# VectorE's order in the gated feed-forward loops: the product of gate and up half first, then the low part of the next weights, then the product's low part, then the side step

## The reference, cut to what matters

```
def swiglu(a, w13, w2):
    gate, up = jnp.split(a @ w13, 2, axis=-1)
    return (jax.nn.silu(gate) * up) @ w2
...
        mod = c_act @ ada_w[l] + ada_b[l]
        (sh1, sc1, gt1, sh2, sc2, gt2, sh3, sc3, gt3) = jnp.split(mod, N_ADA, axis=-1)
        f = swiglu_2(modulate_2(rmsnorm(h, ln_ffn1[l]), sh1, sc1), ffn1_wg[l], ffn1_wu[l], ffn1_wd[l])
```

## Time and profile before

| what | value |
|---|---|
| median of 3 runs | 2943.21 us (2938.38 to 2951.15) |
| the profiled execution | 2962.52 us |
| its span in the trace | 2961.2 us |
| PE busy | 2783.0 us, 94% of the span |
| DVE busy | 2008.7 us, 68% |
| ACT busy | 1226.4 us, 41% |
| POOL busy | 340.5 us, 11% |
| mean granted TensorE clock | 0.967 of full speed |
| mean transfer rate | 177 GB/s |

### The profile page before, as it was taken

How to read it: one execution, slowest core, us unless ns; L and a number is a source line. 1 busy time by engine, 2 the same in 40 slices (tenths; PEclk the granted TensorE clock), 3 DMA queues, 4 the chain that set the end, 5 groups by cost and what they waited for, 6 DMA issues and landing times.

```text
span 2961.2 us, 61219 instructions
## 1 busy us (share of the span) xinstructions
PE 2783.0 (94%) x26612; PEld 2633.2 (89%) x26612; DVE 2008.7 (68%) x2888; ACT 1226.4 (41%) x1634; POOL 340.5 (11%) x332
## 2 busy tenths in 40 slices
PE   7999998999999998988999989999999998989999
PEld 5888886999998777987999888999999998988998
DVE  5787776777776787677656865676565577647654
ACT  2323224445444334434544432555454444144643
POOL 5000001202011121003110020021020101000301
PEclk9999998999999998998998999999999999999999
DMA  8355353899996776998656622456576664233664
GB/s 291 115 188 162 107 172 101 243 257 283 256 267 190 209 232 190 264 285 220 185 166 163 158 73 87 115 157 185 166 200 173 176 165 107 87 103 119 178 168 132
DMA packets 747401, 525.17 MB, mean 177 GB/s; under 512 B 19370, under 2 KB 711788, under 8 KB 747004
## 3 DMA queue, kind: packets, MB, share of 16 engines
q1 hardware_dynamic: 741808, 515.87, 60.8%
q0 software_dynamic: 4128, 5.06, 0.6%
q10 hardware_dynamic: 1196, 0.32, 0.0%
HBM read 520.07 MB, written 2.94 MB: 177 GB/s over the span
## 4 chain that ended last, share of the span: by engine, by line
PE 40%; DVE 9%; ACT 6%; issue 5%; DMA 1%; POOL 0%; DVEq 0%; SPq 0%; ACTq 0%; POOLq 0%
PE bank L519 11%; PE bank L520 11%; PE bank L521 11%; ACT weights_hi L487 4%; DVE weights_lo L498 2%; DVE conv_out L2374 1%; PE bank L2548 1%; PE bank L2540 1%; PE bank L2552 1%; PE bank L1520 1%; PE bank L548 1%; DMA weights_raw<-in_ffn_w 1%; DVE side_sums_odd L620 0%; DVE side_sums L620 0%; DVE conv_out L2371 0%
## 5 line engine op out<-in xcount | busy, mean ns | idle before, releaser
L498 DVE TENSOR_TENSOR weights_lo<-weights_raw,weights_hi 128x2048 fp32r<-128x2048 f32 (+3 forms) x414 | 852.8, 2060 | 367.9 <-ACT weights_hi L487 367.6
L487 ACT ACTIVATE weights_hi<-weights_raw 128x2048 fp32r<-128x2048 f32 (+3 forms) x414 | 709.7, 1715 | 596.9 <-PE bank L521 479.7
L519 PE MATMUL bank<-ffn_in_hi,weights_hi 128*128 128x256 f32 x1184 | 340.9, 288 | 28.1 <-DVE ffn_prod L1388 17.5
L520 PE MATMUL bank<-ffn_in_lo,weights_hi 128*128 128x256 f32 x1184 | 334.2, 282 | 0.0
L521 PE MATMUL bank<-ffn_in_hi,weights_lo 128*128 128x256 f32 x1184 | 333.9, 282 | 0.0
L519 PE MATMUL bank<-mix_in_hi,weights_hi 128*128 128x256 f32 x960 | 280.5, 292 | 11.0 <-DVE conv_in L2404 4.4
L519 PE MATMUL bank<-mac_in_hi,weights_hi 128*128 128x256 f32 x1024 | 288.5, 282 | 2.2 <-DVE mac_prod L2157 1.7
L520 PE MATMUL bank<-mac_in_lo,weights_hi 128*128 128x256 f32 x1024 | 287.6, 281 | 0.0
L521 PE MATMUL bank<-mac_in_hi,weights_lo 128*128 128x256 f32 x1024 | 287.6, 281 | 0.0
L520 PE MATMUL bank<-mix_in_lo,weights_hi 128*128 128x256 f32 x960 | 272.7, 284 | 0.0
L521 PE MATMUL bank<-mix_in_hi,weights_lo 128*128 128x256 f32 x960 | 272.3, 284 | 0.0
(11 more groups left out here) (437 smaller groups left out, 7008.0 us busy)
## 6 DMA issues: line engine op xcount, KB each, us to landing
weights_raw<-in_ffn_w SPq DMA_DIRECT2D x132, 512.0 KB, 6.4
weights_raw<-in_w_in SPq DMA_DIRECT2D x120, 512.0 KB, 5.1
side_weights<-in_ada_w SPq DMA_DIRECT2D x86, 576.0 KB, 4.4
weights_raw<-in_ffn_wg SPq DMA_DIRECT2D x88, 512.0 KB, 4.0
weights_raw<-in_ffn_wu SPq DMA_DIRECT2D x88, 512.0 KB, 5.3
weights_raw<-in_ffn_wd SPq DMA_DIRECT2D x64, 704.0 KB, 4.6
weights_raw<-in_ffn_w SPq DMA_DIRECT2D x48, 704.0 KB, 7.2
side_weights<-in_ada_w SPq DMA_DIRECT2D x112, 256.0 KB, 3.2
```

The costliest lines, as they stand in the source:

```text
L487: k.s.activation(k.w_hi[i % HIGHS][:, 0:n], k.raw[s % RING][:, 0:n], ACT.Copy).then_inc(*k.hi.up())
L498: k.v.tensor_tensor(k.w_lo[s % RING][:, 0:n], k.raw[s % RING][:, 0:n], k.w_hi[i % HIGHS][:, 0:n].bitcast(F32), ALU.subtract).then_inc(*k.l ...
L519: k.te.matmul(out, l[0], r[0], start=first, stop=False)
L520: k.te.matmul(out, l[0], r[1], start=False, stop=False)
```

## The change: what it does

Two loops of VectorE change their order; no instruction is added or removed, and the other engines' queues stay as they are. In `dve_ffn_up` an iteration was: low part of the weights, side steps, product, product's low part. It becomes: product, low part of the weights, product's low part, side steps. In `dve_macaron` the same is done from iteration 6 on, without side steps; iterations 0 to 5 keep their order.

```
 def dve_ffn_up(k, sides, other):
     v = k.v
     for i in range(KF):
-        dve_lo(k)
-        for _ in range(sides.up[i]):
-            dve_side(k)
         v.wait_ge(*k.gated.at(i + 1))
         v.wait_ge(*k.mid_lo.at(i - 1))
         v.tensor_tensor(k.prod[i % 2][:, :], k.gate[i % 2][:, :], k.GB[ffn_turn(k, i) % 2][0][:, T:2 * T],
                         ALU.mult).then_inc(*k.ev.up())
+        dve_lo(k)
         v.wait_ge(k.ev.h, ffn_turn(k, i) + 1)
         v.wait_ge(*k.mid_hi.at(i + 1))
         v.tensor_tensor(k.mid[1][:, i, :], k.prod[i % 2][:, :], k.mid[0][:, i, :].bitcast(F32),
                         ALU.subtract).then_inc(*k.mid_lo.up())
+        for _ in range(sides.up[i]):
+            dve_side(k)
         if i in sides.up_end:
             dve_side_finish(k, sides.up_end[i], k.GB[0][1])
...
     for i in range(KF):
-        dve_lo(k)
+        if i < LATE:
+            dve_lo(k)
         if i == 0:
             dve_rms(k)
...
         if i >= LATE:
             v.wait_ge(*k.gated.at(i + 1))
             v.tensor_tensor(x, g, bank[1][:, 0:T], ALU.mult).then_inc(*k.ev.up())
+            dve_lo(k)
             v.wait_ge(k.ev.h, turn + 1)
             v.wait_ge(*k.mid_hi.at(i + 1))
             v.tensor_tensor(k.mid[1][:, i, :], x, k.mid[0][:, i, :].bitcast(F32), ALU.subtract).then_inc(*k.mid_lo.up())
```

## The result

The changed kernel takes 2906.86 us (median; 2899.46 to 2908.98), the kernel before 2941.16 us beside it: ratio 0.987, 95% interval 0.9846 to 0.9895, a gain of 34 us by the medians and of 38 by the ratio. A later comparison of the same two gave 0.9885 (0.9864 to 0.9907), 33 us. The recorded forecast was 2919 us, a gain of 24: the sign and the first block as the place were right, but the gain is some 40% larger than said, and 2906.86 lies just outside the range (2907 to 2938).

What follows compares the result with a forecast made beforehand. A chain between VectorE and ScalarE, 0.67 us longer than TensorE's 5.44, bounds the first block's slow stretches. Gains of 6.4, 7.1, 5.3 and 5.1 make 24 us: 2943.2 - 24 = 2919 us, range 2907 to 2938.

Steps and rivals of the forecast that it cites:

- The ring of 6.11 us: First block's up loops: VectorE and ScalarE hand one chain back and forth, 6.11 us per iteration against TensorE's 5.44.
- Rival 1: First block's up loops: transfers hold the old pace at 265 GB/s, gaining only 3.8 us, 2939 us; chance 0.17.
- Rival 2: First block: only TensorE's visible waits for the product, 17.5 us, come back, 2926 us; chance 0.09.
- Rival 3: First block: new ring over three iterations is longer if landings exceed 10.5 us; 19 us slower, 2962 us; chance 0.06.
- third layer, double, 4 slabs: End of third layer's up loop, two side steps per iteration: 6.4 us a slab instead of 7.68, gaining 5.1 us.
- third layer, 7 slabs "gain nothing": Third layer stretch where TensorE already runs at 5.44 us a slab, 38.08 us in all: no gain.
- the transfers 6.4: Third layer's double side steps: 2.23 MB per iteration takes 6.4 us at 350 GB/s, taken as each slab's time.
- VectorE's bound 6.06: Third layer's double side steps: VectorE's instruction durations per iteration add up to 6.06 us.
- I cost this half of the change at nothing: Second block: low part was done before SiLU anyway and TensorE has no wait worth naming, so gain 0.
- rival 4: Second block also falls into the faster pace: 17 us on top of the forecast, 2902 us; chance 0.05.
- the middle of 5.44 and 5.71: TensorE's pace without waits in the first block's single-side-step stretches: 5.575 us a slab, both ends giving the range.
- To some 0.1 us each: First block: ScalarE's wait for the product was to fall from 3.4 us to this per iteration.

Runs made afterwards that it cites:

- e3: Kernel before, with only the first block's side step moved behind the product's low part; weights' low part stays ahead of the product: 2911.49 us, ratio 0.9895.

## Why the prediction was wrong by 12 us

Two of the 12 us are not the change's: the kernel before measured 2943.2 us when the forecast was made and 2941.16 beside the result. As a gain the range was 5 to 36 us and 34 lies inside it; in the later comparison the changed kernel's median was 2914.28. That 2906.86 falls just outside the range rather than just inside is chance. That the middle was 10 us too small is not.

**What held.** The ring of 6.11 us was the cause: taking only the side step out of it gives the gain, within the intervals (e3). TensorE's wait for the product vanished, and the list of waits shows the ring cut. *Rival 1* (transfers hold the pace) fell: the four stretches run at 277 to 315 GB/s, above the 265 it named, and TensorE has no wait for weights in them. *Rival 2* (only the visible 17.5 us) fell: the four stretches gave 29.5. *Rival 3* fell: ScalarE's waits for raw weights rose from 87.0 to 126.5 us in the whole span, but none reaches TensorE. One landing took 10.8 us (500 to 650 us, median 6.5), longer than the 10.5 at which this rival was to decide; a single one did no harm. The bound from the transfers does exist, as the layout with more double side steps shows.

**The terms of the sum**, in the two profiled executions:

| term | forecast (ends) | measured |
|---|---|---|
| first layer, 15 slabs | 6.4 (4.4 to 8.4) | 92.92 - 85.09 = 7.8 |
| second layer, 18 slabs | 7.1 (4.6 to 9.5) | 110.52 - 101.35 = 9.2 |
| third layer, single, 10 slabs | 5.3 (4.0 to 6.7) | 61.94 - 57.44 = 4.5 |
| third layer, double, 4 slabs | 5.1 (1 to 5.5) | 30.70 - 22.68 = 8.0 |
| third layer, 7 slabs "gain nothing" | 0 | 38.08 - 39.58 = -1.5 |
| second block | 0 | 3 to 10 (experiments) |

The first block's terms add up to 28 us, against 24. Over the profiles its three up loops take 413 us together in the old order and 386 in the new: 27 us. Timed apart, this half gave 0.9881 and 0.9911, some 26 to 35 us.

**Step one that failed: the third layer's double side steps.** I took "the transfers 6.4" and "VectorE's bound 6.06" as what each of these four slabs must take. The term was 5.1 us and measured 8.0. Both bounds are rates of a long run. Five raw slabs and three side buffers are a stock, and six iterations don't use it up: measured are 5.44 us a slab and one side sum. With twelve such iterations the last slabs did take 6.33 (6.1 to 6.4 was said), at 348 GB/s. The Trainium skill, page "DMA: Bandwidth & Descriptors", section "Bandwidth", has about 358 GB/s from HBM for one core; the highest rows of this case, 348 here and 350 in the earlier trace rows, agree. That a longer run of such iterations would stay at 6.3 us is to be expected, but no run here is long enough to show it. VectorE's 6.06 was too high by itself: it was a sum of durations, and from start to start such an iteration is 1261.81 - 1255.38 less 0.81 of waiting, 5.6 us, in the kernel with more of them. The term had slips of its own: it left out this stretch's side sum, without which 6.4 us a slab would have given a gain of 4.2, and 30.70 - 4 x 6.06 is 6.5, not 5.5. And the row of 350 GB/s, read as made of transfers under 1 MiB, has three of 1 MiB issued within it; the row that shows such a rate with smaller transfers alone is the one of 348.

**Step two: "I cost this half of the change at nothing"**, and rival 4's "nothing in the profile speaks for it". I looked at an iteration in the middle of the loop, where TensorE indeed waits for nothing. The place that mattered is the loop's start, iteration 6: the new order lengthens TensorE's stand ahead of slab 8 from 0.1 to 0.3 us to 0.4 to 0.6, and the pace is set as it goes on. In place of nothing, this half gave 3 to 10 us. Rival 4 named the outcome, but not that it is a draw in each execution, in both orders: its 17 us, which counted the up loops alone, would need all four layers to go from slow to fast, and by the counts the change brings four in ten of them.

**Smaller ones.** The pace: the middle of 5.44 and 5.71 was fair, since both paces occur in the new order (the first layer nearly all at 5.44, the third at 5.65 for 17 slabs); the 5.71 itself is 5.65 a slab and the stands at slabs 6 to 8, spread over 16. "To some 0.1 us each" for ScalarE's wait was careless: it always waits out the product itself, 0.55 us per iteration measured; nothing hung on it. And the profiled execution before, which I took 20 us above the median as a mere offset, was one in which all four layers of the second block had drawn the slower pace. By the counts 1.2 of four are fast in the old order, so that explains some 6 of the 20 us.

## What to carry to other kernels

When two engines hand one chain back and forth and neither is full, add up the chain from start to start; what stands in it without belonging to it can be moved behind it, as the side step was here at no cost. A bound worked out as a rate applies only after the buffers' stock is used up, so count the iterations that it lasts. And compare stages between several profiles before a stage's difference is put down to an edit: here the second block alone can differ by 20 us from execution to execution (four layers of 5), in either order.

## What the runs showed of the hardware

In these loops TensorE's matmuls of 128x256 run at one of two paces at the full granted clock, 113.3 or 117.8 ns apart (7 slabs are 336 matmuls: 38.08 us in the earlier trace rows, 39.58 after). The pace holds as long as TensorE works through such matmuls without a stand, for some 1200 of them behind slab 8, and is set anew when it starts again; equal pauses made it alternate. It can also change at a side sum: with more double side steps 7 slabs run at 5.44 us, and behind the next side sum they run at 5.65. What decides it is not to be seen in the trace.

A layer of the second block differs by 5 us by it. That is not all that sets executions of one kernel apart. The second block's half took 2930.88 us in one profiled execution and 2950.96 in another, with four and two fast layers, which is 10 us. Another stretch differs by as much: the same work of the first block behind its first two feed-forward layers, all engines, in these two executions.

```profile
904.70:1088.81 184.11, 168.44 (x1628) 149.63 (x1628) 145.01 (x207) 68.16 (x117) 32.64 (x39) 0.98 0.71 207
905.31:1100.12 194.81, 176.15 (x1627) 153.79 (x1628) 147.25 (x207) 68.49 (x117) 32.24 (x39) 0.93 0.67 197
```

The granted clock was 0.98 there in the faster execution and 0.93 in the slower one.
